# Root by Sqrt and one Newton step, root applied in the transposing matmul, prologue, boundaries and small vectors rearranged

## The reference

```python
def rms_norm(x, gain):
    y = x * lax.rsqrt(jnp.mean(x * x, axis=-1, keepdims=True) + RMS_EPS)
    return y * gain
def swiglu_ffn(h, w_in, w_out):
    g, u = jnp.split(h @ w_in, 2, axis=-1)
    return (jax.nn.silu(g) * u) @ w_out
for i in range(DEPTH):
    mod = jax.nn.silu(c) @ w_ada[i] + b_ada[i]
    sh1, sc1, g1, sh2, sc2, g2, sh3, sc3, g3 = jnp.split(mod, 9, axis=-1)
    h = rms_norm(x, norm_pre[i, 0]) * (1 + sc1) + sh1
    x = x + 0.5 * g1 * rms_norm(swiglu_ffn(h, w_ffn_in[i, 0], w_ffn_out[i, 0]), norm_post[i, 0])
    h = rms_norm(x, norm_pre[i, 1]) * (1 + sc2) + sh2
    x = x + g2 * rms_norm(hybrid_mixer(h, ...), norm_post[i, 1])
    h = rms_norm(x, norm_pre[i, 2]) * (1 + sc3) + sh3
    x = x + 0.5 * g3 * rms_norm(swiglu_ffn(h, w_ffn_in[i, 1], w_ffn_out[i, 1]), norm_post[i, 2])
return x
```

## Time and profile before

| what | us |
|---|---|
| median of three runs | 1622.02 (1617.34 to 1626.06) |
| the profiled execution | 1622.57 |
| its span | 1620.8 |
| PE busy | 1566.1 (97%) |
| VectorE busy | 1115.6 (69%) |
| ACT busy | 735.9 (45%) |
| granted TensorE clock, mean of the span | 0.989 |

### The profile page before, as it was taken

How to read it: one execution, slowest core, us unless ns; L and a number is a source line. 1 busy time by engine, 2 the same in 40 slices (tenths; PEclk the granted TensorE clock), 3 DMA queues, 4 the chain that set the end, 5 groups by cost and what they waited for, 6 DMA issues and landing times.

```text
span 1620.8 us, 24562 instructions
## 1 busy us (share of the span) xinstructions
PE 1566.1 (97%) x10210; PEld 1417.8 (87%) x10210; DVE 1115.6 (69%) x1371; ACT 735.9 (45%) x878; POOL 164.9 (10%) x96
## 2 busy tenths in 40 slices
PE   6899999999999999999999999999999999999997
PEld 3898988998988888999889998799989888889986
DVE  4767857466897877676676766638678878665454
ACT  2334434456563444444344443336656544454442
POOL 1000000502320110000000000022224002000000
PEclk9999999999999999999999999999999999999999
DMA  9869864555676763787737877356456777545562
GB/s 352 270 212 324 288 201 147 170 154 149 203 247 225 255 208 118 259 282 258 268 127 264 273 260 270 99 176 200 146 174 200 254 243 247 168 145 184 184 190 91
DMA packets 197554, 343.76 MB, mean 212 GB/s; under 512 B 18722, under 2 KB 110130, under 8 KB 197444
## 3 DMA queue, kind: packets, MB, share of 16 engines
q1 hardware_dynamic: 197444, 342.21, 64.5%
HBM read 341.11 MB, written 1.05 MB: 211 GB/s over the span
## 4 chain that ended last, share of the span: by engine, by line
PE 81%; DVE 10%; DMA 3%; SPq 2%; ACT 2%; issue 2%; POOL 0%; DVEq 0%; ACTq 0%; POOLq 0%
PE ps L630 10%; PE ps L633 10%; PE ps L632 9%; PE ps L927 6%; PE ps L928 6%; PE ps L929 6%; PE ps L648 5%; PE ps L647 5%; PE ps L646 5%; PE ps L976 4%; PE ps L978 4%; PE ps L977 4%; DVE w_lo L1262 2%; DMA ada_slab<-in_w_ada 2%; DVE ada_acc L1282 1%
## 5 line engine op out<-in xcount | busy, mean ns | idle before, releaser
L1262 DVE TENSOR_TENSOR w_lo<-w_raw,w_hi 128x1024 fp32r<-128x1024 f32 x480 | 614.4, 1299 | 174.8 <-ACT w_hi L1038 174.1
L1038 ACT ACTIVATE w_hi<-w_raw 128x1024 fp32r<-128x1024 f32 x490 | 508.2, 1052 | 387.5 <-DMA w_raw<-in_w_ffn_in 113.7
L630 PE MATMUL ps<-h_hi,w_hi 128*128 128x256 f32 x1408 | 402.2, 286 | 7.8 <-ACT h_hi L1074 4.3
L633 PE MATMUL ps<-h_hi,w_lo 128*128 128x256 f32 x1408 | 399.6, 284 | 0.0
L632 PE MATMUL ps<-h_lo,w_hi 128*128 128x256 f32 x1376 | 389.9, 283 | 0.0
L630 PEld LDWEIGHTS ps<-h_hi,w_hi 128*128 128x128 f32 x1408 | 272.7, 194 | 9.2 <-ACT h_hi L1074 4.5
L633 PEld LDWEIGHTS ps<-h_hi,w_lo 128*128 128x128 f32 x1408 | 272.5, 194 | 0.0
L632 PEld LDWEIGHTS ps<-h_lo,w_hi 128*128 128x128 f32 x1376 | 264.8, 192 | 1.0 <-issue 1.0
L1282 DVE SCALAR_TENSOR_TENSOR ada_acc<-ada_slab,c_silu,ada_acc 128x1024 f32<-128x1024 f32 x128 | 187.4, 1464 | 58.4 <-DMA ada_slab<-in_w_ada 58.1
L976 PE MATMUL ps<-h_hi,w_hi 128*128 128x256 f32 x704 | 204.5, 291 | 4.8 <-DVE xbc L1482 3.3
L977 PE MATMUL ps<-h_lo,w_hi 128*128 128x256 f32 x704 | 201.5, 286 | 0.0
(11 more groups left out here) (246 smaller groups left out, 1903.4 us busy)
## 6 DMA issues: line engine op xcount, KB each, us to landing
w_raw<-in_w_ffn_in SPq DMA_DIRECT2D x176, 512.0 KB, 4.7
w_raw<-in_w_in SPq DMA_DIRECT2D x168, 512.0 KB, 3.7
ada_slab<-in_w_ada SPq DMA_DIRECT2D x128, 512.0 KB, 4.7
w_raw<-in_w_ffn_out SPq DMA_DIRECT2D x88, 512.0 KB, 3.6
...
```

The lines of the kernel that those rows point to most:

```text
L630: mm(out, wh[:, cs], HH[:, k, :], start=(k == 0 and t == 0), stop=False)
L633: ins = mm(out, wl[:, cs], HH[:, k, :], start=False, stop=(c != 0 and k == KD - 1 and t == 1))
L1038: fn(WH[:, n % N_HI, 0:width], RAW[:, n % N_RAW, 0:width], ACT.Copy).then_inc(w_hi, 1)
L1262: dve.tensor_tensor(WL[:, n % N_RAW, 0:width], RAW[:, n % N_RAW, 0:width], WH[:, n % N_HI, 0:width], ALU.subtract).then_inc(w_lo, 1)
```

## The change

- The root: ACT computes `root` = Sqrt(sum / 1024 + eps) behind its squares (with an Identity between the two halves that makes the first half's part). VectorE takes the reciprocal and one Newton step.
- The root no longer multiplies the rows. `x_scale` makes y_tok = x times the scale row, which needs no root; `x_diagonal` multiplies the 128x128 identity by the root, and h_turn multiplies by that diagonal in place of the identity. `x_square` writes its squares to PSUM, y_tok being in use.
- A 128x1 Sqrt (`DUMMY`) ahead of the y squares of each boundary.
- Boundaries: VectorE makes x_scale, root and diagonal of tokens 0 ahead of the next w_lo. Ahead of a SwiGLU block h_lo of tokens 0 goes behind the diagonal of tokens 1. A mixer on PE starts with half chunks 0 and 1, then gate sums, shifts and h_turn of tokens 1, then half chunks 2 and 3.
- Prologue: slabs 0 to 7, then x, then 8 to 15; h_turn ahead of the shifts; ACT splits two chunks (not seven) ahead of h_hi.
- Small vectors: one table made on the host, one DMA at chunk 30 of sub-layer 0, the two large constants at chunks 40 and 50, no transpose.
- The result is stored in four halves, not two rows of tiles.

```diff
+            small_inputs = [(VECS[:], vecs_d, small_landed), (KC[:, P:K_DEC], consts_d[:, P:K_DEC], small_landed),
+                            (KC[:, K_DEC:K_N], consts_d[:, K_DEC:K_N], dec_landed)]
...
-            first_slab(8)
...
-            for i in range(1, 8):
+            for i in range(1, ADA_FIRST):
                 first_slab(i)
-                first_slab(8 + i)
-                if i == 3:
+                if i == 7:
...
-                    if s == 0 and c >= 4 and later:
-                        dst, src, sig = later.pop(0)
+                    if s == 0 and c in (30, 40, 50):
+                        dst, src, sig = small_inputs[(c - 30) // 10]
...
+            def h_turn(b, tt, first=False):
+
+                pe.wait_ge(f_ok.sem, f_ok.at(b, tt + 1))
                 for half in range(2):
-                    pe.wait_ge(f_ok.sem, f_ok.at(b, 2 * tt + half + 1))
...
             def mixer(s):
                 layer = s // 3
+                shifts(s, 0)
+                h_turn(s, 0)
                 pe.wait_ge(yg_ok.sem, yg_ok.at(s - 1, 4))
-                pe.wait_ge(hl_ok.sem, hl_ok.at(s, 2))
+                pe.wait_ge(xsq_ok.sem, xsq_ok.at(s, 4))
                 for j in range(4):
+                    if j == 2:
+                        gate_row_sums(s)
+                        shifts(s, 1)
+                        h_turn(s, 1)
+                    if j % 2 == 0:
+                        pe.wait_ge(hl_ok.sem, hl_ok.at(s, j // 2 + 1))
                     token_chunk(BASE[s] + j, j, 6, HH, HL, KD, (0,), range(2))
-                h_turn(s, 1)
...
-            shifts(0, 0)
-            shifts(0, 1)
-            pe.wait_ge(ident_landed, 16)
-            h_turn(0, 0)
+            h_turn(0, 0, first=True)
+            h_turn(0, 1, first=True)
+            shifts(0, 0, last=True)
+            shifts(0, 1, last=True)
...
+                fn(DUMMY[:], one, ACT.Sqrt)
                 y_square(s + 1, 0)
...
+            def refined(nh, r, t, tt):
+
+                chain(dve.reciprocal(r, RT[:, tt:tt + 1]))
+                chain(dve.scalar_tensor_tensor(t, r, nh, r, ALU.mult, ALU.mult))
+                chain(dve.scalar_tensor_tensor(r, t, 1.5, r, ALU.add, ALU.mult))
...
+            def x_diagonal(b, tt):
...
+                dve.tensor_scalar(DG[:, tt, :], ident, RB[:, tt:tt + 1], None, ALU.mult).then_inc(f_ok.sem, 1)
```

More of the change, by code:

```diff
@@ L668, in out_chunks, with shifts @@
                         ins.then_inc(y0_ps.sem, 1)
-            def shifts(b, tt):
+            def shifts(b, tt, last=False):
                 if tt == 0:
@@ L717, in gate_sums, with gate_row_sums @@
                 ins.then_inc(g_ps.sem, 1)
-            def between(b):
-                if b == SUBS:
-                    return
-                shifts(b, 0)
-                h_turn(b, 0)
-                shifts(b, 1)
+            def gate_row_sums(b):
                 pe.wait_ge(yg_ok.sem, yg_ok.at(b - 1, 2))
+                pe.wait_ge(xsq_ok.sem, xsq_ok.at(b, 2))
                 gate_sums(b)
@@ L756, in ffn @@
                 out_chunks(s, N_IN, KF, AH, AL, before)
-                between(s + 1)
             def scores(q, k, h):
@@ L1057, in y_square @@
                     fn(PS[:, 2 + half, :], PS[:, 4 + n, :], ACT.Square, accum_out=SY[:, n:n + 1]).then_inc(ysq_ok.sem, 1)
+                    if half == 0:
+                        act.wait_ge(ysq_ok.sem, ysq_ok.at(s, n + 1))
+                        fn(SV[:, tt:tt + 1], SY[:, n:n + 1], ACT.Identity, scale=1.0 / D, bias=EPS[:]).then_inc(part_ok.sem, 1)
+                act.wait_ge(ysq_ok.sem, ysq_ok.at(s, 2 * tt + 2))
+                act.wait_ge(part_ok.sem, parts(s + 1, 0, tt))
+                fn(RT[:, tt:tt + 1], SY[:, 2 * tt + 1:2 * tt + 2], ACT.Sqrt, scale=1.0 / D, bias=SV[:, tt:tt + 1])\
+                    .then_inc(yrt_ok.sem, 1)
             def x_square(b, tt):
@@ L1370, in boundary @@
                     return
+                x_scale(b, 0)
+                x_root(b, 0)
+                x_diagonal(b, 0)
                 split_to(BASE[b] + 1)
-                x_root(b, 0)
-                x_norm(b, 0)
                 y_gate(b, 1)
                 x_update(b, 1)
-                h_lo(b, 0)
-                x_root(b, 1)
-                x_norm(b, 1)
                 if b % 3 == 1:
+                    h_lo(b, 0)
+                    x_scale(b, 1)
+                    x_root(b, 1)
+                    x_diagonal(b, 1)
                     split_to(BASE[b] + 3)
+                else:
+                    x_scale(b, 1)
+                    x_root(b, 1)
+                    x_diagonal(b, 1)
+                    h_lo(b, 0)
                 h_lo(b, 1)
@@ L1641, in _ @@
             dve.sem_inc(ada_used.sem, 8)
-            for i in range(8, 12):
-                ada_step(0, i)
             x_root(0, 0)
             x_root(0, 1)
-            for i in range(12, ADA_FIRST):
+            for i in range(8, 11):
                 ada_step(0, i)
             scale_row(0, 4)
-            x_norm(0, 0)
-            x_norm(0, 1)
+            x_scale(0, 0)
+            x_diagonal(0, 0)
+            x_scale(0, 1)
+            x_diagonal(0, 1)
+            for i in range(11, ADA_FIRST):
+                ada_step(0, i)
             split_to(0)
@@ L1653, in _ @@
             h_lo(0, 1)
+            split_to(3)
             for s in range(SUBS):
```

180 lines of the change are left out of this document (97 added, 83 removed).

## The result

The changed kernel takes 1608.7 us (median of 9, 1603.6 to 1612.3), the kernel before 1626.1 beside it (median of 9, 1617.3 to 1630.8). The ratio is 0.9895, 95% interval [0.9875, 0.9914]: faster by 1.05%. The prediction had the direction, but 1608.7 lies above its range (1590 to 1606). The profiled executions stand at 1622.57 (span 1620.8) and 1608.68 (span 1606.9), so 13.9 us of the span went where I had summed 26.0. The medians lie 17.4 us apart: the execution that the sum was made against (1622.57) was one of the quicker ones of the kernel before.

What follows compares the result with a forecast made beforehand. TensorE, busy for 97% of the span, bounds the kernel, so only its idle time or lower clock can be won. Terms 12.6 + 2.8 + 4.3 + 5.1 + 1.2 = 26.0 us off 1622.57 gave 1596.6 us, range 1590 to 1606.

Steps and rivals of the forecast that it cites:

- Boundaries 2, 3 and 5: Boundaries before SwiGLU sub-layers 2, 3 and 5: TensorE's wait for scaled rows and slow h_turns go; gain 12.6 us.
- Mixer boundaries: The two boundaries before a mixer: one 2.7 us wait, then work without a gap; 1.4 us each, 2.8 in sum.
- Rival B: The clock falls in the new waits of two mixers and before the prologue's last shifts: 1601 us, chance 0.08.
- Prologue: Before the first sub-layer: TensorE starts 2.7 us earlier and 1.6 us of low clock is absorbed; gain 4.3 us.
- Sub-layer 0: TensorE's 3.48 us stop for a w_lo and 1.6 us of lower clock behind it go; gain 5.1 us.
- The end: From TensorE's end to the last store: shorter root and halved stores gain 1.2 us, bounds 0.5 and 2.
- the sum itself: Whole kernel: gains at boundaries, prologue, sub-layer 0 and end add to 26.0 us, taken from 1622.57 us.
- Rivals A: Sub-layer 0 is fed by the DMA engines, keeps its stall and hands back the prologue's gain: 1606 us, chance 0.18.
- Rival C: ScalarE table loads are exposed wherever they stand on its queue, nine of 1.28 us: 1608 us, chance 0.03.
- D: Slower than before: ScalarE-to-VectorE hand-over at 12 places; 2.2 us extra each cancels the gain; 1627 us, chance 0.03.
- E: Boundaries do not shorten because something other than the root is next; half of 15.4 us lost: 1604 us, chance 0.08.
- signs of being wrong: A TensorE wait for w_lo in sub-layer 0, or ScalarE's Identity and Sqrt above 0.5 us each with hand-over.

Runs made afterwards that it cites:

- e12: e11 with the old root (bit seed, three Newton steps on VectorE; no Identity, Sqrt or Sqrt table loads on ScalarE): 1608.6 us, ratio 0.9896.
- e15: e11 without the small Sqrt ahead of the y squares of each boundary: 1596.9 us, a single time.
- e6: The changed kernel with a pad of 64 bytes a partition directly ahead of the work tiles: 1610.0 us.
- e10: Changed kernel at old places, but act_hi alone moved in sub-layer 0, act_lo alone in 2, both in 3 (512 bytes higher) and 5: 1605.1 us, one time.
- e14: e11 with 64 bytes left free at the very front, so every tile moves and no distance between tiles changes: 1596.9 us.
- e4: The kernel before with only the small-vector table: one transfer at chunk 30, large constants at chunks 40 and 50, no transposes: 1620.9 us, ratio 0.9961.
- e16: e11 with 64 bytes of pad ahead of the work tiles and the prologue's two x_scale on GpSimd instead of VectorE: 1593.9 us, ratio 0.9803.
- e2: The changed kernel with every tile common to both kernels back at its old place, same instructions and order: 1601.1 us, ratio 0.9842.
- e3: The kernel before with an unread pad of 1120 bytes a partition, putting later tiles where the changed kernel has them: 1631.0 us, ratio 1.0033.
- e11: The changed kernel with common tiles at their old places and a mixer's gate sums run behind its first h_turn: 1592.3 us, ratio 0.9794.

## Why the prediction was wrong, step by step

- **Boundaries 2, 3 and 5: right.** 12.6 forecast, 12.85 measured. Waits gone, h_turn 2.05 (forecast 1.95), root 0.96 (1.05). The reason was incomplete: e12 shows that the root carries 3.0 of the 4.7 us, half of it through tokens 0, and e15 that ScalarE's squares of tokens 1 are the next limit.
- **Mixer boundaries: direction right, size off.** 2.8 forecast, 4.05 measured. The wait was 2.28 us, not 2.7 (chunks 0 and 1 start 6.02 us behind the first shifts, 6.3 forecast), and from there to chunk 2 it took 8.0 us where I had 8.2; the remaining 0.2 a boundary was in my rounding of what follows. Rival B's loss of 1.6 each is real in other executions; with it the term is 0.9.
- **Prologue: mis-sized.** 4.3 forecast, 2.94 measured. L628 starts at 41.56, not 40.4. VectorE's roots ended as summed (22.98 for 22.9), but eight ada steps took 1.36 us each where I had put 1.24, so the last one ended at 37.87 instead of 36.8. The full clock came as said, the granted clock being 1.00 from 36 to 44 us, but not in every execution: where it fell (e6, e10, e12, e14, e15) some 1.6 us of the gain went, as rival B had it.
- **Sub-layer 0: size right, cause not isolated.** 5.1 forecast, 4.60 measured and 5.65 with the table alone; 0.6 of what lies between the two is a longer wait for the gate sums (2.4 us, 1.8 before). The prediction leaned on d_skip, whose issue held SP for 4.18 us, but the three other d_skip transfers of that kernel were issued in 0.61 to 1.02 us. e4 takes away all eighteen and spaces the large ones, so which of them made the stall is not shown.
- **The end: mis-sized.** 1.2 forecast, 0.4 measured. That is below its bounds (0.5 to 2). The root gave 0.9 (x_update starts 2.69 us behind y_gate, 3.58 before). The halved stores gave nothing: the last one is issued 1.44 us behind the start of x_update, 1.45 before, and from there to the end it took 3.54 us, 3.06 before. That last stretch varies (2.47 in e12 and e16); why is open.
- **The step that failed: the sum itself.** It took everything outside the edited places as unchanged. The change's list of tiles is an edit too: it moved act_hi from the distance 192 to 32, which costs 4.65 us in the outputs of the SwiGLU sub-layers and 1.9 in the mixers' last part, 6.5 together (e2, e3, e10). The term for it was put at nothing without a reason, and no rival contained it.
- **The second loss: the mixers' middle**, 4.4 us, of which the lower clock is 3.4 (by windows of 2 us it costs 6.8 before and 10.2 after in the two mixers) and waits 0.9. The lower clock turns up in the mixers in every kernel run here, at changing places, and costs 6.8 to 10.2 us in both together, boundaries apart; why it was 10.2 in this execution and 6.8 in e11 stays open.

With the outputs at their old speed the time would have been 1602, inside the range (e2 measured 1601.1); the clock in the mixers is 3.4 of the 5.6 us that separate that from 1596.6. Rivals A, C, D and E did not come: D's wait for ScalarE's Sqrt at the boundaries is 0.16 us, where it needed 2.2. Rival C's 1608 is what was measured, but by chance: its mechanism, the exposed table loads, is refuted by e15. Neither of the prediction's signs of being wrong came, no wait for w_lo in sub-layer 0 and Identity and Sqrt at 0.29 to 0.30 us; both looked at the edited places alone, where the sum held.
